# Activating the prompt's expert dot products in pairs on ScalarE, in the first of two PEER layers

## The chip, the cores and the metric

One core of a Trainium2 chip runs the whole program. The metric is the device time of one execution in microseconds (us). A slot, below, is one retrieved expert for each of 128 tokens; PE is TensorE, DVE is VectorE, ACT is ScalarE, POOL is GpSimd, SP is SyncE.

## What is computed

Two layers of a trunk run over five tiles of 128 tokens: four of the sample, one of the prompt. Each layer has a mixer (layer 0: HGRN2 and attention; layer 1: an RG-LRU block) and then a PEER retrieval. The change is in the retrieval of layer 0, which for a tile of 128 tokens and 8 heads computes

```
q = (xb @ w_q);  s1, s2 = q halves @ keys;  top 16 of the 16 x 16 sums -> eidx, g = softmax(sc)
act = gelu(einsum('thkd,td->thk', u[eidx], xb))
return einsum('thk,thkd->td', (g * act), v[eidx])
```

So each head and tile (a unit) has 16 slots. For a slot, a row of `u` and a row of `v` are gathered for every token, the dot product of the `u` row with the token is taken, its gelu times the gate weighs the `v` row, and the weighed rows are summed.

## The kernel before

All five engines run programs written out in order; there is no scheduler. 1280 slots (640 to a layer) go through the same pipeline, slot `g` being `g // 16` in units. In layer 0 slots 0 to 511 belong to the sample (8 heads x 4 tiles) and slots 512 (`SAMPLE`) to 639 (up to `SPAN` = 640) to the prompt, 16 to a head. Below, the stage is these 128 slots of the prompt, and "slot 26" means the 26th of the stage, g = 538.

For each slot POOL gathers 128 rows of 8 KB into one place of a ring (L1227). In the stage the ring has only 6 places, because the rest of it holds work of the next mixer; a place is free when PE has used it (`slot_free`). DVE takes the dot products (L1731, `dots`). ACT applies gelu (`gelu(g)`, L1315, `acts`). In the stage ACT then also multiplies by the gate (L1321, `prods`) and spreads the result on the diagonal of a 128 x 128 matrix (L1325, `diag`, four buffers); both are `weight(g)`. Outside the stage DVE makes the diagonal in one instruction (L1740). PE multiplies the diagonal with the gathered `v` rows and adds up in PSUM (L2062, 8 matmul instructions to a slot). In the stage PE takes slots in pairs: at every odd slot it runs `accumulate(g - 1)` and `accumulate(g)`, one after the other, each waiting for its own diagonal.

Between slots every engine runs background steps of the next mixer, each at a written slot number, in a generator called `background()`; a step due at slot g comes after that engine's own work of slot g. In the stage the background is:

- slots 0 to 8: the end of the last sample tile of layer 0 (ACT: `end_root_mean_square` L1259 at slot 4, `store_end` L1275 at slot 8; PE: `end_turn` L2001 at slot 7);
- from slot 9 to about 80: four blocks, n = 0 to 3, of the RG-LRU over the sample, 16 slots apart. PE multiplies the inputs (L2099) and the gates (L2118). ACT copies out the inputs (L1348, L1355; slots 13 and 15 of block 0), applies gelu to the gate branch (L1401; slots 18 and 21), sigmoid (L1367; slots 23 and 25), exp and tanh (L1376, L1377) and the first squares (L1384) at slot 26, the other squares at slot 28, and sqrt (L1390) at slots 29 and 30. Block n has the same steps 16n slots later. DVE multiplies, scans and forms the output (L1809 to L1846);
- slots 80 to 127: the projection of three sample tiles (PE L1975, two to eight k steps between pairs; its weights L1183 are loaded by SP as the scans let go of their room), and for each tile a residual (DVE L1631, L1633), root mean square (ACT L1250 to L1254, slots 87, 103 and 119), norm (DVE L1639 to L1645, a slot later), transposes (PE L1988, slots 89, 105 and 121), the copy of these (ACT L1268, slots 90, 106 and 122) and queries (PE L2014, slots 91 and 92, 107 and 108, 123 and 124).

An ACT instruction of a function that isn't in the loaded table set has an ACT_TABLE_LOAD before it. In this kernel gelu, sigmoid, exp (with tanh) and sqrt each bring one when another of the four ran before; copies, squares and multiplications bring none. ACT also computes the softmax's exp for each unit (`exponent`, L1297, at slot 5 of a unit in the stage).

Of the kernel before, what the change touches and what calls it, by code (L numbers as in the profile page):

```python
# [23 lines left out]
ACT = mybir.ActivationFunctionType  # L24
# [917 lines left out]
def unit_of(u):  # L942

    layer, v = divmod(u, HEADS * NB)
    return (layer,) + (divmod(v, SB) if v < HEADS * SB else (v - HEADS * SB, SB))
# [13 lines left out]
def ends_tile(u):  # L959
    layer, h, b = unit_of(u)  # L960
    return h == HEADS - 1


def ends_sum(u):
    layer, h, b = unit_of(u)
    return b < SB or h == HEADS - 1


def made_by_act(g):
    return SAMPLE <= g < SPAN  # L970


def diags_before(g):

    lo, hi = SAMPLE, SPAN
    by_act = min(max(g, lo), hi) - lo
    return by_act if made_by_act(g) else g - by_act
# [28 lines left out]
def route_steps(u):  # L1006

    return (2, 4, 6, 8, 10) if u < SB else (0, 1, 3, 5, 7)


def end_steps(u):

    return (1, 3, 4, 6, 7, 8) if u == HEADS * SB else (3, 7, 9, 12, 14, 15)


def trunk(nc, X, HY, HT, ident, iota16, io):
    def body(sb, ps, sem):
# [26 lines left out]
        dots, acts, prods = (sb(n, [P, 2 * TOPK]) for n in ("dots", "acts", "prods"))  # L1044
# [51 lines left out]
        dot_done, act_done, diag_v, diag_a, prod_done = (sem(n) for n in ("dot_done", "act_done", "diag_v", "diag_a", "prod_done"))  # L1096
# [44 lines left out]
        with nc.Block() as block:  # L1141
# [91 lines left out]
            def _(act):  # L1233
# [22 lines left out]
                def end_root_mean_square(e):  # L1256
                    b, n = e % NB, 2 * NB + e
                    act.wait_ge(added, add_of(e // NB * HEADS * NB + (HEADS - 1) * SB + b if b < SB else (e // NB + 1) * HEADS * NB - 1) + 1)
                    act.activation(HY[:, b, :], X[:, b, :], ACT.Square, accum_out=ss[:, n:n + 1]).then_inc(e_squared, 1)  # L1259
                    act.wait_ge(e_squared, e + 1)  # L1260
                    act.activation(rt[:, n:n + 1], ss[:, n:n + 1], ACT.Copy, scale=1.0 / D, bias=EPS).then_inc(e_shifted, 1)
                    act.wait_ge(e_shifted, e + 1)
                    act.activation(rt[:, n:n + 1], rt[:, n:n + 1], ACT.Sqrt).then_inc(e_rooted, 1)
# [7 lines left out]
                def store_end(e):  # L1271
                    b = e % NB
                    act.wait_ge(e_turned, e + 1)
                    for k in range(KD):
                        last = act.activation(HT[:, k, b * P:(b + 1) * P], qp[:, k * P:(k + 1) * P], ACT.Identity,  # L1275
                                              scale=AB1[:, 0, cond_of(b), k:k + 1], bias=AB1[:, 1, cond_of(b), k:k + 1])
                    last.then_inc(e_stored, 1)
# [17 lines left out]
                def exponent(u):  # L1295
                    act.wait_ge(top_ready, u + 1)
                    act.activation(expo[:, :], top[:, :], ACT.Exp, bias=negtop[:, 0:1],  # L1297
                                   accum_out=total[:, 0:1]).then_inc(exp_done, 1)

                def unpack(u):  # L1300
                    a = add_of(u)
                    act.wait_ge(slot_free, (u + 1) * TOPK)
                    act.wait_ge(added, a)
                    if u == HEADS * NB - 1:
                        act.wait_ge(l_y, KD)
                    for r in range(2):
                        for c in range(2):
                            last = act.activation(tmp[r * HALF:(r + 1) * HALF, c * 512:(c + 1) * 512],  # L1308
                                                  acc[acc_of(u)][c * HALF:(c + 1) * HALF, r * 512:(r + 1) * 512], ACT.Copy)
                    last.then_inc(unpacked, 1)  # L1310

                def gelu(g):
                    act.wait_ge(dot_done, g + 1)
                    j = g % (2 * TOPK)
                    act.activation(acts[:, j:j + 1], dots[:, j:j + 1], ACT.Gelu_apprx_tanh).then_inc(act_done, 1)  # L1315

                def weight(g):
                    u, j = g // TOPK, g % (2 * TOPK)
                    act.wait_ge(gate_ready, u + 1)
                    act.wait_ge(act_done, g + 1)  # L1320
                    act.activation(prods[:, j:j + 1], acts[:, j:j + 1], ACT.Copy,  # L1321
                                   scale=gate[:, u % 2, g % TOPK:g % TOPK + 1]).then_inc(prod_done, 1)
                    act.wait_ge(prod_done, diags_before(g) + 1)
                    act.wait_ge(slot_free, g - NDIAG + 1)
                    act.activation(diag[:, g % NDIAG, :], ident[:, :], ACT.Copy, scale=prods[:, j:j + 1]).then_inc(diag_a, 1)  # L1325
# [277 lines left out]
                    due = next(rest, None)  # L1603
                for g in range(SLOTS_IN_ALL):
                    u, s = divmod(g, TOPK)
                    gelu(g)
                    if made_by_act(g):
                        weight(g)
                    if s == end_steps(u)[0] and u and ends_sum(u - 1):
                        unpack(u - 1)  # L1610
                    if s == route_steps(u)[3] and u + 1 < UNITS:
                        exponent(u + 1)
                    if u and ends_tile(u - 1) and ends_sum(u - 1):
                        e = unit_of(u - 1)[0] * NB + unit_of(u - 1)[2]
                        if s == end_steps(u)[2]:
                            end_root_mean_square(e)
                        if s == end_steps(u)[5] and e < NB:
                            store_end(e)
                    while due is not None and due <= g:
                        due = next(rest, None)  # L1620
# [789 lines left out]
```

## Time and profile before

| what | us |
|---|---|
| timed runs, median (lowest, highest) of 3 | 4360.12 (4358.41, 4360.19) |
| the profiled execution | 4355.29 |
| its span, first to last instruction | 4353.6 |
| busy: PE, DVE, ACT, POOL | 3097.8, 3114.9, 1325.1, 1525.2 |
| DMA: mean rate over the span | 343 GB/s |

All queries below are of this one profiled execution; its times are counted from the span's start. A line of the timeline gives start, duration, engine and line, what is written from what, the count of instructions merged, and in brackets the idle time of the engine before it with what ended it. TensorE's granted clock is 1.00 for 2.4 GHz and 0.50 for 1.2 GHz. The stage lies between about 2130 and 2590 us.

### The profile page before, as it was taken

The numbers are of one execution on the slowest core, as the hardware profiler recorded it, in microseconds if no ns is written. First come the engines' busy times: TensorE is split into PE (matmuls) and PEld (weight loads), VectorE is DVE, ScalarE is ACT, GpSimd is POOL, SyncE is SP. The second block draws the span as 40 slices with busy tenths as digits, with TensorE's granted clock in tenths as the row PEclk, the third lists the DMA queues.
The fourth block names the chain that finished last, engine by engine and source line by source line (L and its number), as shares of the span: only waits on it lengthen the run. The fifth ranks groups of instructions, "written<-read, shape, count | busy, mean of one in ns | idle before, by whom it ended". The sixth has DMA issues, their size and how long they took to land.

```text
span 4353.6 us, 47679 instructions
## 1 busy us (share of the span) xinstructions
PE 3097.8 (71%) x15504; PEld 1117.7 (26%) x15504; DVE 3114.9 (72%) x7566; ACT 1325.1 (30%) x3008; POOL 1525.2 (35%) x1310
## 2 busy tenths in 40 slices
PE   7698887776667667666699786657566576666665
PEld 2266564221111111111133231122221211221111
DVE  6633333678878888788767677878779787778776
ACT  5432142222212222122467642232323322222111
POOL 0000000344444444444333334434344344434442
PEclk9899968898778878777799888788888898876766
DMA  8511002899999999999888999999999999999997
GB/s 332 202 38 42 34 1 106 325 364 420 420 421 420 417 411 412 410 411 411 346 326 304 361 361 392 420 394 416 387 398 407 392 419 420 421 410 417 418 410 313
DMA packets 227796, 1494.28 MB, mean 343 GB/s; under 512 B 25016, under 2 KB 48360, under 8 KB 55400
## 3 DMA queue, kind: packets, MB, share of 16 engines
q0 software_dynamic: 184320, 1342.26, 75.9%
q1 hardware_dynamic: 35364, 133.37, 8.1%
q10 hardware_dynamic: 7884, 15.87, 1.0%
q8 instruction: 111, 1.82, 0.2%
q14 instruction: 117, 0.96, 0.1%
HBM read 1488.02 MB, written 3.38 MB: 343 GB/s over the span
## 4 chain that ended last, share of the span: by engine, by line
DMA 30%; DVE 20%; PE 18%; issue 10%; ACT 4%; POOL 1%; DVEq 0%; ACTq 0%; POOLq 0%
DMA trunk_ring<-in_uv,trunk_index 27%; PE trunk_acc L2062 9%; DVE trunk_ring L1731 5%; DVE trunk_diag L1740 3%; DMA trunk_wbuf<-in_w_lru 2%; PE trunk_qp L1975 2%; POOL trunk_ring L1227 1%; PE trunk_qp L2099 1%; DVE trunk_onehot L1702 1%; DVE trunk_onehot L1706 1%; DVE trunk_pick L1709 1%; PE trunk_q L2099 1%; PE trunk_acc L2099 1%; DVE trunk_work L1667 1%; ACT L1315 1%
## 5 line engine op out<-in xcount | busy, mean ns | idle before, releaser
L2062 PE MATMUL trunk_acc<-trunk_ring,trunk_diag 64*64 64x512 f32 x10240 | 1717.6, 769 | 1045.1 <-DVE trunk_diag L1740 973.8
L1227 POOL DMA_INDIRECT trunk_ring<-in_uv,trunk_index x1280 | 1513.1, 1182 | 2304.3 <-PE trunk_acc L2062 1940.3
L1731 DVE CUSTOM_DVE_ANT_0 trunk_ring<-trunk_ring,HY 128x1024 f32<-128x1024 f32 x1280 | 1562.8, 1223 | 537.1 <-DMA trunk_ring<-in_uv,trunk_index 514.2
L1315 ACT ACTIVATE trunk_acts<-trunk_dots 128x1 f32<-128x1 f32 x1280 | 257.1, 202 | 2303.3 <-DVE trunk_dots L1731 2299.7
L2062 PEld LDWEIGHTS trunk_acc<-trunk_ring,trunk_diag 64*64 64x64 f32 x10240 | 337.2, 155 | 2248.5 <-DVE trunk_diag L1740 1930.4
L1740 DVE TENSOR_SCALAR trunk_diag<-ident,trunk_acts,trunk_gate 128x128 f32<-128x128 f32 x1152 | 396.5, 344 | 104.7 <-ACT trunk_acts L1315 104.6
L2021 PE MATMUL trunk_qp<-HT,trunk_wbuf 128*128 128x512 f32 x448 | 274.7, 697 | 0.0
L1315 ACT ACT_TABLE_LOAD x137 | 175.8, 1283 | 2.4
L1308 ACT ACTIVATE trunk_tmp<-trunk_acc 64x512 f32<-64x512 f32 x264 | 155.5, 589 | 6.1 <-PE trunk_acc L2062 3.2
L2021 PEld LDWEIGHTS trunk_qp<-HT,trunk_wbuf 128*128 128x128 f32 x448 | 72.9, 204 | 215.4 <-issue 215.4
L1975 PE MATMUL trunk_qp<-trunk_ring,HY 128*128 128x512 f32 x224 | 109.1, 621 | 0.0
L2099 PE MATMUL trunk_q<-HT,trunk_wbuf 128*128 128x128 f32 (+1 forms) x304 | 63.0, 367 | 60.8 <-DMA trunk_wbuf<-in_w_lru 60.8
L1731 DVE DVE_READ_ACCUMULATOR2_ANT trunk_dots<- 128x1 f32 x1280 | 105.7, 83 | 0.0
L2014 PEld LDWEIGHTS trunk_q<-HT,trunk_wbuf 128*128 128x128 f32 x768 | 97.6, 206 | 30.2 <-issue 28.9
L446 POOL COPY hgrn_Vm<-hgrn_V 64x640 f32<-64x640 f32 x8 | 5.7, 718 | 278.9 <-ACT hgrn_V L476 278.7
L1297 ACT ACT_TABLE_LOAD x80 | 102.6, 1283 | 1.4
L2014 PE MATMUL trunk_q<-HT,trunk_wbuf 128*128 128x128 f32 x768 | 101.7, 292 | 1.1 <-ACT HT L1268 1.1
L248 DVE TENSOR_TENSOR mod_w_lo<-mod_wmod,mod_w_hi 128x4096 fp32r<-128x4096 f32 x16 | 70.8, 4425 | 35.9 <-DMA HY<-in_norm_g 16.9
L289 PE MATMUL mod_modp<-mod_w_hi,mod_cond_hi 128*2 128x512 f32 x192 | 77.0, 401 | 14.2 <-ACT mod_w_hi L220 14.2
L1748 DVE TENSOR_TENSOR trunk_tmp<-trunk_tmp,trunk_G 128x1024 f32<-128x1024 f32 x66 | 80.6, 1222 | 5.3 <-ACT trunk_tmp L1308 5.3
L1750 DVE TENSOR_TENSOR X<-X,trunk_tmp 128x1024 f32<-128x1024 f32 x66 | 80.9, 1225 | 2.3
L835 DVE CUSTOM_DVE_ANT_0 att_LG<-att_A,att_band 128x384 f32<-128x384 f32 (+2 forms) x40 | 22.3, 558 | 83.5 <-PE att_A L892 83.5
(319 smaller groups left out, 3396.1 us busy)
## 6 DMA issues: line engine op xcount, KB each, us to landing
mod_wmod<-in_w_mod SPq DMA_DIRECT2D x16, 2048.0 KB, 8.0
trunk_wbuf<-in_w_q SPq DMA_DIRECT2D x24, 1024.0 KB, 9.2
trunk_ring<-in_uv,trunk_index POOLq DMA_INDIRECT x1280, 17.5
HT<-in_w_mod SPq DMA_DIRECT2D x8, 2048.0 KB, 8.3
trunk_wbuf<-in_w_lru SPq DMA_DIRECT2D x16, 1024.0 KB, 18.6
trunk_wbuf<-in_w_rg SPq DMA_DIRECT2D x8, 1024.0 KB, 14.3
hgrn_wqvg<-in_w_hgrn_qvg SPq DMA_DIRECT2D x4, 1536.0 KB, 6.3
hgrn_wfb<-in_w_hgrn_fb SPq DMA_DIRECT2D x4, 1024.0 KB, 4.9
```

Source lines behind the costliest of these rows:

```text
L1227: pool.indirect_dma_start(ring[:, slot, :], None, uv[:, :], bass.IndirectOffsetOnAxis(ap=index[:, u % 2, s:s + 1], axis=0), element_offset ...
L1297: act.activation(expo[:, :], top[:, :], ACT.Exp, bias=negtop[:, 0:1], accum_out=total[:, 0:1]).then_inc(exp_done, 1)
L1308: last = act.activation(tmp[r * HALF:(r + 1) * HALF, c * 512:(c + 1) * 512], acc[acc_of(u)][c * HALF:(c + 1) * HALF, r * 512:(r + 1) * 512 ...
L1315: act.activation(acts[:, j:j + 1], dots[:, j:j + 1], ACT.Gelu_apprx_tanh).then_inc(act_done, 1)
L1731: dve.tensor_tensor_reduce(u_rows, u_rows, HY[:, b, :], 1.0, 0.0, ALU.mult, ALU.add, dots[:, j:j + 1]).then_inc(dot_done, 1)
L1740: dve.tensor_scalar(diag[:, g % NDIAG, :], ident[:, :], acts[:, j:j + 1], gate[:, u % 2, g % TOPK:g % TOPK + 1], ALU.mult, ALU.mult).then_ ...
L1750: dve.tensor_tensor(X[:, b, :], X[:, b, :], tmp[:, :], ALU.add).then_inc(added, 1)
L1975: last = pe.matmul(dst[:, lo:lo + 512], HY[:, b, k * P:(k + 1) * P], weights_of(k)[:, lo:lo + 512], start=(k == 0), stop=(k == KD - 1), sk ...
L2014: last = pe.matmul(q0[:, half * P:(half + 1) * P], wq[:, k * 2 * P + half * P:k * 2 * P + (half + 1) * P], HT[:, k, b * P:(b + 1) * P], st ...
L2021: return pe.matmul(qp[:, half * LS:(half + 1) * LS], wq[:, k * 2 * P + half * P:k * 2 * P + (half + 1) * P], HT[:, k, 0:LS], start=(k == 0 ...
L2062: last = pe.matmul(acc[acc_of(u)][c * HALF:(c + 1) * HALF, r * 512:(r + 1) * 512], diag[rows, g % NDIAG, rows], ring[rows, slot, D + c * 5 ...
L2099: last = pe.matmul(psum(i), w[:, k * 2 * P + c * P:k * 2 * P + (c + 1) * P], HT[:, k, tokens], start=(k == 0), stop=(k == KD - 1), skip_gr ...
```

## The change

ACT's `gelu` gets a count `n`: it waits for the dot products of slots g to g + n - 1, activates n adjacent columns in one instruction and signals `act_done` n times. Outside the stage n is 1 and nothing changes. In the stage ACT does nothing for its own slot at an even slot; at an odd slot it runs one `gelu` over two columns and then `weight` for the even and for the odd slot. The background steps, `unpack`, `exponent` and the rest keep their places in the loop. A step due at an even slot of the stage now runs before the gelu and the weight of that slot instead of after. No other engine's program changes.

```
-                def gelu(g):
-                    act.wait_ge(dot_done, g + 1)
+                def gelu(g, n=1):
+                    act.wait_ge(dot_done, g + n)
                     j = g % (2 * TOPK)
-                    act.activation(acts[:, j:j + 1], dots[:, j:j + 1], ACT.Gelu_apprx_tanh).then_inc(act_done, 1)
+                    act.activation(acts[:, j:j + n], dots[:, j:j + n], ACT.Gelu_apprx_tanh).then_inc(act_done, n)
...
                 for g in range(SLOTS_IN_ALL):
                     u, s = divmod(g, TOPK)
-                    gelu(g)
-                    if made_by_act(g):
+                    if not made_by_act(g):
+                        gelu(g)
+                    elif g % 2:
+                        gelu(g - 1, 2)
+                        weight(g - 1)
                         weight(g)
```

## Rows read from the trace of the kernel before

**Rows 1.** Windows: the stage; length, busy PE, PEld, DVE, ACT, POOL, clock, DMA share, GB/s

```profile
2130.00:2590.00 460.00, 389.03 (x1677) 146.31 (x1678) 315.78 (x675) 286.92 (x627) 153.01 (x128) 0.90 0.89 333
```

**Rows 2.** Waits within the stage: engine, line, waited for: total us, times, longest

```profile
ACT trunk_acts L1315 <- DVE trunk_dots L1731: 110.5, 46, 7.3
...
PEld trunk_acc L2062 <- ACT trunk_diag L1325: 107.5, 38, 9.5
```

**Rows 3.** Group of instructions within the stage: count, busy us, mean ns, idle before

```profile
L1315 ACT ACT_TABLE_LOAD x28 | 35.9, 1283 | 0.5
```

**Rows 4.** Timeline of ACT in block 0, slots 26 and 27 of the stage

```profile
2224.92 1.28 ACT L1315 ACT_TABLE_LOAD   x1
...
2227.26 1.28 ACT L1376 ACT_TABLE_LOAD   x1
...
2235.91 0.20 ACT L1315 ACTIVATE trunk_acts<-trunk_dots 128x1 f32<-128x1 f32 x1
...
2236.54 0.40 ACT L1325 ACTIVATE trunk_diag<-ident,trunk_prods 128x128 f32<-128x128 f32 x1
```

**Rows 5.** Timeline of PE in block 0, from before slot 26 to slot 29

```profile
2225.99 5.42 PE L2099 MATMUL trunk_qp<-HT,trunk_wbuf 128*128 128x512 f32 x12
2231.34 1.09 PE L2062 MATMUL trunk_acc<-trunk_ring,trunk_diag 64*64 64x512 f32 x8
2236.99 1.98 PE L2062 MATMUL trunk_acc<-trunk_ring,trunk_diag 64*64 64x512 f32 x8 [4.56 <-ACT trunk_diag L1325]
2238.90 5.97 PE L2099 MATMUL trunk_qp<-HT,trunk_wbuf 128*128 128x512 f32 x12
2244.81 1.95 PE L2062 MATMUL trunk_acc<-trunk_ring,trunk_diag 64*64 64x512 f32 x16
```

**Rows 6.** Timeline of POOL, DVE, SP and PE in and behind block 3, to slot 84

```profile
2423.05 0.94 POOL L1227 DMA_INDIRECT trunk_ring<-in_uv,trunk_index  x1 [1.50 <-PE trunk_acc L2062]
...
2430.85 4.65 PE L2062 MATMUL trunk_acc<-trunk_ring,trunk_diag 64*64 64x512 f32 x24 [8.61 <-ACT trunk_diag L1325]
...
2442.20 1.22 DVE L1731 CUSTOM_DVE_ANT_0 trunk_ring<-trunk_ring,HY 128x1024 f32<-128x1024 f32 x1
...
2452.11 0.81 SPq L1183 DMA_DIRECT2D trunk_ring<-in_w_out  x2
...
2461.62 3.70 PE L1975 MATMUL trunk_qp<-trunk_ring,HY 128*128 128x512 f32 x8
```

**Rows 7.** DMA issues from 2400 to 2600 us: count, median us to landing

```profile
trunk_ring<-in_uv,trunk_index POOLq DMA_INDIRECT x63, 7.9
```

**Rows 8.** Timeline of PE at the second projected tile, slots 103 to 108

```profile
2517.72 1.99 PE L2062 MATMUL trunk_acc<-trunk_ring,trunk_diag 64*64 64x512 f32 x8 [2.45 <-ACT trunk_diag L1325]
...
2525.49 1.98 PE L2062 MATMUL trunk_acc<-trunk_ring,trunk_diag 64*64 64x512 f32 x8 [0.66 <-ACT trunk_diag L1325]
2527.41 1.97 PE L1988 MATMUL trunk_qp<-ident,HY 128*128 128x128 f32 x8
...
2531.40 1.09 PE L2062 MATMUL trunk_acc<-trunk_ring,trunk_diag 64*64 64x512 f32 x8 [0.59 <-ACT trunk_diag L1325]
2532.42 3.84 PE L2014 MATMUL trunk_q<-HT,trunk_wbuf 128*128 128x128 f32 x32
```

**Rows 9.** Timeline of ACT at the same tile: slots 103 and 105

```profile
2516.65 0.20 ACT L1315 ACTIVATE trunk_acts<-trunk_dots 128x1 f32<-128x1 f32 x1 [2.52 <-DVE trunk_dots L1731]
...
2517.58 1.04 ACT L1250 ACTIVATE HY<-X 128x1024 f32<-128x1024 f32 x1
...
2524.41 0.20 ACT L1315 ACTIVATE trunk_acts<-trunk_dots 128x1 f32<-128x1 f32 x1 [1.62 <-DVE trunk_dots L1731]
```

**Rows 10.** Windows of PE alone: start:end, length, busy (instructions), granted clock, DMA, GB/s

```profile
2517.00:2520.00 3.00, 1.99 (x8) 0.50 0.98 410
```

**Rows 11.** Timeline of DVE and ACT at the stage's entrance, slots 3 and 4

```profile
2143.08 1.23 DVE L1750 TENSOR_TENSOR X<-X,trunk_tmp 128x1024 f32<-128x1024 f32 x1
...
2146.41 1.04 ACT L1259 ACTIVATE HY<-X 128x1024 f32<-128x1024 f32 x1
```

## The prediction

> **What bounds the kernel now.** I read four views, all in the stage, since no program outside it changes. The windows: the stage is 460 us of the span, DMA busy at 0.89 and PE for 389 us [rows 1]. A wait taken out of it can therefore shorten it, and what is won or lost is kept, because the gathers behind the stage are issued as the ring comes free. The waits: PE's weight loads wait 107.5 us for ACT's diagonals, at 38 places, and ACT's gelu waits 110.5 us for DVE's dot products, at 46 [rows 2]. So PE hangs on ACT, but ACT has two reasons to be late: its own queue (then fewer instructions help) or a late dot product (then a gelu that waits for two dots makes the first of them later). The groups: in the stage gelu brings 28 table loads of 1283 ns, 35.9 us [rows 3], while one gelu takes 0.20 [rows 4]. The timeline of ACT and PE shows which reason holds where.
>
> **Part 1, what the pairs remove in an RG-LRU block (four times).** At slot 26 of block 0 the sigmoids are done when the gelu load begins at 2224.92. Gelu and weight of slot 26 follow, then the exp load at 2227.26. Exp, tanh and squares run, then a gelu load again, gelu 27 at 2235.91 and its diagonal at 2236.54 [rows 4]. In the change the exp step, due at the even slot 26, follows the sigmoids directly: no gelu load between, all 2227.26 - 2224.92 = 2.34 us earlier. The sqrt steps at slots 29 and 30 lose two more loads in the same way. That is three loads of 1.28 a block, 12 in all, 15.4 us of ACT.
>
> What reaches PE is less. Before, slot 26 was used at 2231.34, 4.56 us of idle followed, and slot 27 ran from 2236.99 [rows 5]. After, gelu for both starts at 2235.91 - 2.34 = 2233.57. The diagonal of 26 starts 0.63 behind it, as 2236.54 - 2235.91 shows, and ends 0.40 later at 2234.60; PE starts 0.05 after, at 2234.65. The diagonal of 27 costs a second `weight`, 0.64, and is hidden: PE needs about 1 us for slot 26. PE's idle shrinks only from 4.56 to 2234.65 - (2225.99 + 5.42) = 3.24, as slot 26 no longer runs ahead. Behind the idle before, 8 matmuls took 1.98 instead of 1.09 and the next 12 took 5.97 instead of 5.42: 1.44 lost to the lower clock [rows 5]. I take the same loss after 3.24 of idle. Both slots, the 12 matmuls and that loss, 1.88 + 5.35 + 1.44 with the overlaps of the rows taken off, end at 2243.3 to 2243.4; before it was 2244.81. Gain 1.4. Ends: 2.9 if the clock doesn't fall after the shorter idle; 0.3 if slots 26 and 27 both run at 1.98. From there PE is busy without a gap to the next block, so the two sqrt loads reach nothing. Blocks 0, 1 and 2 alike: **-4.2 (-8.7 to -0.9)**.
>
> Block 3 has no inputs of a next block behind it, so PE waits for ACT throughout and all three loads lie on that chain. But slot 74 is now used only with slot 75, and its place in the ring is let go late. Before, its gather (of slot 80) went out at 2423.05 [rows 6]. PE ran slot 75 from 2430.85, after 8.61 of idle [rows 6]; after, it starts 74 and 75 at 2430.85 - 2.34 = 2428.5, at 1.98 each, and the place of 74 is free at 2430.5, the gather out 0.8 later. Gathers here land after 7.9 us [rows 7], so 2439.2, just before DVE, whose work follows ACT's squares and moves with them, is free for slot 80 at about 2439.7; it was 2442.20. The last scans and outputs follow that dot, then the load of the last projection rows at 2452.11, then their matmuls at 2461.62 [rows 6]. So the end of block 3 gains at most 2.5, and nothing if the landing takes 3 us longer: **-1.8 (-2.6 to 0)**.
>
> A switch of tables here costs 1.28 and the next ACTIVATE follows directly [rows 4]. The Trainium skill (ScalarE: Activation LUTs, What ACT_TABLE_LOAD costs) adds about 1.38 us of drain to each. That drain is not visible in this trace; with it, three blocks would give an estimated 4.1 us more and the sum below would be about 0.7.
>
> **Part 2, what the pairs add at the projected tiles (three times).** Here ACT waits for dots, and the path runs through it: residual, root mean square, norm, transposes, copy, queries. The new wait is the gelu's for the odd dot; behind it on ACT are both weights and then the step of the tile, and PE's pair and POOL's gathers into the places of both slots wait for those. Three delays add up.
>
> First, ACT's L1250 followed the weight of slot 103 [rows 9]. Now two weights lie between the gelu at 2516.65 and L1250, +0.64, and DVE's norm and the dot of 105 wait for that. Second, slot 104, which PE had done before slot 105 (0.66 of idle between [rows 8]), now shares the gelu of 105. Gelu came at 2524.41 and PE at 2525.49, 1.08 later [rows 8, 9]; after, gelu at 2525.05, slot 104 on PE at 2526.13, slot 105 behind it, each 1.98 at the clock of these rows. The transposes start at 2530.0 instead of 2527.41: +2.6 so far. Third, the copy of the transposes is due at the even slot 106 and now precedes the gelu of 106. Slot 106, which ran in the shadow of the copy, follows it with slot 107 (was 2531.40), another +1.0 at full clock. The queries (2532.42) start 3.6 later. Behind them PE is busy on projections until the next tile, so the delay is kept. Ends: 2.7 if the longer run of slots 104 and 105 brings the clock back before the transposes (8 instructions in nearer 1.09 than 1.97 [rows 5, 8]); 5.4 if slots 106 and 107 run at 1.98 and the queries begin at the lower clock. Three tiles: **+10.8 (+8.1 to +16.2)**.
>
> PE idles longer in one piece here: from the end of slot 101 to the gelu of slot 103, where 102 used to run, and again up to 105. After 2.45 of idle slot 103 took 1.99, and the granted clock there was 0.50, the 1.2 GHz level [rows 8, 10]. The Trainium skill (TensorE: Matmul & The Clock Gate, HAM oscillation) warns that every idle gap before a burst may be paid again in slow matmuls; it speaks against this change, and by it the tiles stand at their upper end, which is rival (a).
>
> **Part 3, the entrance.** The root mean square at the even slot 4 waited for slot 4's weight until 2146.41, although its input was ready at 2143.08 + 1.23 = 2144.31 [rows 11]. It now starts 2.06 earlier; the exp and the gelus behind it follow until the dots of slots 5 and 7 limit them, so about 1.1 is left for PE. Against that, the copy at the even slot 8 now precedes slot 8's gelu, and slot 8 moves behind it with slot 9: +1.0 to +1.98 by the rows of the tiles [rows 8]. I take **0 (-1.1 to +1.7)**.
>
> **Nothing for the rest.** In the pairs where PE is busy without a gap, the first diagonal comes where the second used to and the second 0.64 later, behind 1 us of work for the first slot; the cover is PE's backlog, and without it each pair would cost about 1.0. A second column adds nothing that would show in a gelu's 0.20 [rows 4].
>
> **Sum.** -4.2 - 1.8 + 10.8 + 0 = +4.8. From the profiled 4355.29 that is 4360.1. The timed median is 4360.12, 4.8 above the profiled run; on it I forecast 4364.9.
>
> **Rivals.** (a) Slower: the low clock stays over slots 106 and 107 and the start of the queries in all three tiles. Then 16.2 + 1.7 - 4.2 - 1.8 = +11.9, 4372. It decides where slots 106 and 107 take over 3 us together instead of 1.95. For it: 1.98 at four places of one tile or block [rows 5, 8]. Against it: slot 107 already ran in 1.09, behind 0.59 of idle. (b) The change doesn't shed its loads, the gelu load before slot 26 staying where it was. Then 1.28 comes back at each of three blocks, which takes them to about -0.4, and the sum is +8.6 to +10: 4369. Against it: loads stand only where the set changes [rows 4]. (c) Faster: the tiles' delay is covered, because the projections between tiles wait for gathers and not for PE, and the blocks stay at full clock: -8.7 - 2.6 = -11.3, 4349. Against it: PE's rows there have no idle. For it: DMA at 0.89 over the stage [rows 1].
>
> **How the numbers follow.** Forecast 0.58, (a) 0.25, (b) 0.05, (c) 0.12. A measurement of this kernel tells about 0.2%, 8.7 us, from no change. The forecast lies within that, (a) and (b) beyond on the slow side, (c) on the fast side: 0.12 faster, 0.58 same, 0.30 slower. The range takes in the forecast's ends, which with all terms at one side would be -4.3 and +17, and case (a): 4355 to 4377. Only (c) lies outside.
>
> **What would show it.** Right: 20 gelu loads in the stage instead of 28 and four sqrt loads fewer; slots 26 and 27 as one run of 16 matmuls on PE behind some 3.2 of idle; at a tile, L1250 0.6 further behind its gelu, and the queries 3 to 5 us further behind the gelu of slot 103 than 2532.42 - 2516.65 = 15.77. Wrong: L1250 no later behind its gelu, slot 106 still ahead of the copy, or blocks that shorten by over 3 us each. Outside the stage, anything that moves by more than the shift would speak against all of it.

## The result: slower, and the profile after

| what | before | after |
|---|---|---|
| timed runs, median (lowest, highest) of 9 each | 4358.41 (4350.89, 4360.19) | 4377.3 (4372.27, 4400.12) |
| the profiled execution | 4355.29 | 4372.3 |
| its span | 4353.6 | 4370.6 |
| ACT: instructions, busy us | 3008, 1325.1 | 2932, 1292.2 |

After to before is 1.0047, with a 95% interval of 1.0034 to 1.0059: slower, by about 20 us. The forecast was 4364.9 (4355 to 4377), a change too small to be told from none. The profiled execution after is nearly the fastest of its nine, so the profiles differ by less, 17.0 us.

ACT lost what it was to lose: 76 instructions, 64 gelus and 12 table loads. The stage grew all the same, 18.0 us from its first scores to the last. These are lines of the profile after, windows, waits and groups of the stage, which answer to [rows 1 to 3] (line numbers behind L1312 are shifted by one to four).

```profile
2130.00:2610.00 480.00, 393.76 (x1692) 149.04 (x1696) 315.04 (x676) 253.33 (x550) 150.80 (x129) 0.90 0.86 320
```

```profile
PEld trunk_acc L2066 <- ACT trunk_diag L1326: 113.5, 49, 9.5
ACT trunk_acts L1316 <- DVE trunk_dots L1735: 95.5, 28, 7.7
...
ACT L1316 <- DVE trunk_dots L1735: 34.2, 8, 9.3
```

```profile
L1316 ACT ACT_TABLE_LOAD x20 | 25.7, 1283 | 34.4 <-DVE trunk_dots L1735 34.2
```

PE is as busy as before, in a stage that is 18 longer. The new line is the third of the waits: an entry of L1316 without a tile, the table load, which waits for the dot products eight times, 34.2 us. Before, the 28 loads had 0.5 us of idle ahead of them in all [rows 3].

Where the time went can be read off PE's scores (128 x 128 matmuls of `trunk_sc`), one set to a unit of 16 slots. Their distances, from the timelines of PE:

| us between scores | before | after | shift |
|---|---|---|---|
| entrance | 59.28 | 60.13 | +0.85 |
| block 0, block 1, block 2 | 64.49, 64.67, 64.69 | 63.22, 62.88, 63.21 | -4.54 |
| block 3; then projection and tile 1 | 59.31, 52.56 | 54.57, 65.59 | +8.29 |
| tile 2, tile 3 | 47.57, 47.57 | 54.20, 54.35 | +6.63, +6.78 |

The row with +8.29 parts at the end of the projection's last matmuls, 2465.32 before [rows 6] and 2462.35 after: block 3 with the projection lost 2.3, tile 1 lost 5.9. Outside the stage it is -1.6 ahead and +0.6 behind. The 1.6 is scatter: all kernels here run the same program up to the stage, and they reach its first scores between 2129.99 and 2139.19. Together: +17.0, the difference of the two spans.

The timeline of ACT in tile 2 after, beside [rows 9]:

```profile
2514.27 0.31 ACT L1297 ACTIVATE trunk_expo<-trunk_top,trunk_negtop 128x16 f32<-128x16 f32 x1
...
2519.66 1.28 ACT L1316 ACT_TABLE_LOAD   x1 [4.99 <-DVE trunk_dots L1735]
2520.95 0.20 ACT L1316 ACTIVATE trunk_acts<-trunk_dots 128x2 f32<-128x2 f32 x1
...
2522.51 1.04 ACT L1250 ACTIVATE HY<-X 128x1024 f32<-128x1024 f32 x1
...
2529.38 1.28 ACT L1316 ACT_TABLE_LOAD   x1 [4.00 <-DVE trunk_dots L1735]
2530.68 0.20 ACT L1316 ACTIVATE trunk_acts<-trunk_dots 128x2 f32<-128x2 f32 x1
```

The exp of `exponent` is over at 2514.7, ACT idles for 4.99 us, and only then, when the dot has come, the table is loaded. Before, the load ran right behind the exp, inside the idle:

```profile
2510.83 0.19 ACT L1297 ACTIVATION_READ_ACCUMULATOR trunk_expo<-trunk_top,trunk_negtop 128x1 f32 x1
2511.03 1.28 ACT L1315 ACT_TABLE_LOAD   x1
2513.11 0.20 ACT L1315 ACTIVATE trunk_acts<-trunk_dots 128x1 f32<-128x1 f32 x1 [0.79 <-DVE trunk_dots L1731]
```

The timeline of PE at the same tile after, beside [rows 8]: the pair 102 and 103, the pair 104 and 105, transposes, the pair 106 and 107, queries.

```profile
2522.03 3.44 PE L2066 MATMUL trunk_acc<-trunk_ring,trunk_diag 64*64 64x512 f32 x16 [6.02 <-ACT trunk_diag L1326]
2531.76 3.69 PE L2066 MATMUL trunk_acc<-trunk_ring,trunk_diag 64*64 64x512 f32 x16 [6.28 <-ACT trunk_diag L1326]
2535.38 1.09 PE L1992 MATMUL trunk_qp<-ident,HY 128*128 128x128 f32 x8
2538.50 3.50 PE L2066 MATMUL trunk_acc<-trunk_ring,trunk_diag 64*64 64x512 f32 x16 [2.03 <-ACT trunk_diag L1326]
2541.92 3.94 PE L2018 MATMUL trunk_q<-HT,trunk_wbuf 128*128 128x128 f32 x32
```

From the gelu of slot 103 to the transposes it is 14.43 (10.76 before), and from there to the queries 6.54 (5.01 before). From the queries of tile 1 (2487.82; before 2484.85) to that gelu it is 33.13 (31.80). So +1.33, +3.67 and +1.53, in all the 6.5 of this tile.

### The profile page after: what moved, and what is told of

Its sections match the earlier page's. It is cut to its first block, busy times and chain, and to the rows that moved or that the text cites. A ratio compares the mean times of both kernels' runs of the same rounds, so it can differ in the third digit from the quotient of the medians.

```text
span 4370.6 us, 47667 instructions
## 1 busy us (share of the span) xinstructions
PE 3107.1 (71%) x15504; PEld 1119.4 (26%) x15504; DVE 3114.5 (71%) x7566; ACT 1292.2 (30%) x2932; POOL 1526.1 (35%) x1310
## 4 chain that ended last, share of the span: by engine, by line
DMA 30%; DVE 21%; PE 17%; issue 11%; ACT 4%; POOL 1%; DVEq 0%; ACTq 0%; POOLq 0%; SPq 0%
DMA trunk_ring<-in_uv,trunk_index 28%; PE trunk_acc L2066 9%; DVE trunk_ring L1735 5%; DVE trunk_diag L1744 3%; DMA trunk_wbuf<-in_w_lru 2%; PE trunk_qp L1979 1%; POOL trunk_ring L1227 1%; PE trunk_qp L2103 1%; DVE trunk_onehot L1706 1%; DVE trunk_onehot L1710 1%; DVE trunk_pick L1713 1%; PE trunk_q L2103 1%; PE trunk_acc L2103 1%; DVE trunk_work L1671 1%; PE trunk_q L2018 1%
## 5 line engine op out<-in xcount | busy, mean ns | idle before, releaser
L1316 ACT ACTIVATE trunk_acts<-trunk_dots 128x1 f32<-128x1 f32 (+1 forms) x1216 | 244.5, 202 | 2284.2 <-DVE trunk_dots L1735 2282.8
L1316 ACT ACT_TABLE_LOAD x129 | 165.5, 1283 | 36.3 <-DVE trunk_dots L1735 34.2
L2103 PE MATMUL trunk_q<-HT,trunk_wbuf 128*128 128x128 f32 (+1 forms) x304 | 61.6, 362 | 61.5 <-DMA trunk_wbuf<-in_w_lru 61.5
```

The source lines that it names most:

```text
L1316: act.activation(acts[:, j:j + n], dots[:, j:j + n], ACT.Gelu_apprx_tanh).then_inc(act_done, n)
L2103: last = pe.matmul(psum(i), w[:, k * 2 * P + c * P:k * 2 * P + (c + 1) * P], HT[:, k, tokens], start=(k == 0), stop=(k == KD - 1), skip_gr ...
```

## The experiments

Twelve kernels, each timed in several rounds beside the kernel before; ratios are to that kernel, with their 95% intervals. "Distance" is that between scores, as in the table above. Two (e2_count_two, e6_half_rows_single) are the kernel before with one edit; the others are the kernel after, all but e1_count_one with pairs in some slots only, by this edit and a range for `paired`:

```
+def paired(g):
+    return made_by_act(g) and LO <= g - SAMPLE < HI
...
                     if not made_by_act(g):
                         gelu(g)
+                    elif not paired(g):
+                        gelu(g)
+                        weight(g)
                     elif g % 2:
```

### 1. Does the load behind the wait cost the time? (e1_count_one, e2_count_two)

The pair's gelu differs from the single one in two things: it has two columns, and it counts `act_done` up by two. e1_count_one keeps pairs and counts by one:

```
-    act.activation(acts[:, j:j + n], dots[:, j:j + n], ACT.Gelu_apprx_tanh).then_inc(act_done, n)
+    act.activation(acts[:, j:j + n], dots[:, j:j + n], ACT.Gelu_apprx_tanh).then_inc(act_done, 1)
...
-                    act.wait_ge(act_done, g + 1)
+                    act.wait_ge(act_done, acted(g))
```

`acted(g)` is the number of gelus up to that of slot g; DVE's two waits on `act_done` get it too.

> The changed kernel with one difference: a gelu of a pair counts act_done up by one instead of two, and the waits on act_done use the new count. In the built program the table load of a paired gelu then stands ahead of the wait for the dot again, as in the kernel before; pairs, their order and all other work stay. Theory (the loads moved behind the waits): in each of tiles 1 to 3 two loads of 1.28 us go back under the wait, so a tile costs 3.6 instead of 6.2 to 6.8 us against the kernel before, and the entrance about 1.3 less: 7.8 to 9.1 us faster than the changed kernel, about 4368 in the median, still slower than before by some 10. Rival (what the tiles lose is all lateness of the pair and the low clock of TensorE behind it; the loads are off the path): no difference to the changed kernel, 4377.

Measured: 4367.58, 1.0021 (1.0012 to 1.003); against 1.0047 that is 10 to 11 us back, and the intervals don't meet. Its ACT at tile 3, both loads of gelu and the gelus behind them:

```profile
2570.30 1.28 ACT L1326 ACT_TABLE_LOAD   x1
2575.29 0.20 ACT L1326 ACTIVATE trunk_acts<-trunk_dots 128x2 f32<-128x2 f32 x1 [3.70 <-DVE trunk_dots L1748]
...
2579.74 1.28 ACT L1326 ACT_TABLE_LOAD   x1
2583.67 0.20 ACT L1326 ACTIVATE trunk_acts<-trunk_dots 128x2 f32<-128x2 f32 x1 [2.65 <-DVE trunk_dots L1748]
```

The loads run first and the gelu waits. The distances of tiles 2 and 3 are 51.73 and 51.53: 4.2 and 4.0 over the kernel before, where the change has 6.6 and 6.8. So the loads behind the wait cost some 2.6 a tile, 7 to 8 us of the 20 if tile 1 is charged the same, and the rival (no difference) falls. In tile 1 itself only 1.1 came back in this profile, because its pair of slots 90 and 91 and its queries ran more slowly here (2.70 and 4.70 us) than in the change (1.95 and 3.84).

e2_count_two does the opposite: the kernel before, single slots, but a count of two (the waits on `act_done` use the new count).

```
-    act.activation(acts[:, j:j + 1], dots[:, j:j + 1], ACT.Gelu_apprx_tanh).then_inc(act_done, 1)
+    act.activation(acts[:, j:j + 1], dots[:, j:j + 1], ACT.Gelu_apprx_tanh).then_inc(act_done, 2 if made_by_act(g) else 1)
```

> The kernel before, single slots throughout, with one difference: a gelu of the stage counts act_done up by two instead of one, and the waits on act_done use the new count. In the built program all 28 table loads of gelu in the stage then stand behind the wait for the dot. Theory (a load behind a wait costs its 1.28 us only where TensorE's next work hangs on the very dot waited for): at a tile the load before slot 102 delays slot 102 alone, and slot 103, whose dot comes 3 us later, is not delayed; the load before slot 104 finds its dot ready. So the time between the scores of two tiles stays at 47.6 us and the kernel within 3 us of the kernel before. Rival (a load behind a wait costs 1.28 wherever it stands): 2.6 a tile, as with the pairs, and about 8 us or more in all.

Measured: 4358.31, 0.9997 (0.9988 to 1.0006); distances of the tiles 47.68 and 47.96. Its ACT at tile 2:

```profile
2513.42 1.28 ACT L1319 ACT_TABLE_LOAD   x1 [2.07 <-DVE trunk_dots L1735]
2514.71 0.20 ACT L1319 ACTIVATE trunk_acts<-trunk_dots 128x1 f32<-128x1 f32 x1
...
2516.97 0.20 ACT L1319 ACTIVATE trunk_acts<-trunk_dots 128x1 f32<-128x1 f32 x1 [1.24 <-DVE trunk_dots L1735]
```

Here, too, the load waits for the dot, so the count moves it, not the second column. But slot 103's gelu still waits 1.24 for its own dot behind it. With single slots the late load delays only slot 102, which has time. The load becomes dear only when slot 102's load stands in front of slot 103's gelu, and that is what the pair does.

### 2. Which slots lose, which gain? (e4_pairs_tiles, e3_pairs_blocks, e5_pairs_b02)

e4_pairs_tiles: `80 <= g - SAMPLE < 128`. e3_pairs_blocks: `0` to `80`. e5_pairs_b02: `0` to `64`. All count by two, as the change does.

> The changed kernel with pairs only in slots 80 to 127 of the stage (the projected tiles), single slots in the entrance and blocks 0 to 3. Theory: tiles 1 to 3 cost 6.2 to 6.8 us each, 19 us slower than the kernel before, about 4378. Rival, the sum on record: 3.6 each, 10.8 us slower. Second rival (the tiles lose this much only because block 3 handed them a queue of late gathers): under 10 us.

Measured: 4381.96, 1.0054 (1.0041 to 1.0067), 23 us; distances of tiles 2 and 3 54.58 and 54.60, +7.0 each, and +7.2 for the projection with tile 1. The tiles alone carry all of the loss; they lose it without the change in block 3.

> The changed kernel with pairs only in slots 0 to 79 of the stage (entrance, blocks 0 to 3), single slots in the projected tiles (80 to 127). Theory from the shifts between the two traces (entrance +1.4, blocks 0 to 2 -5.1, block 3 +2.3): 1.4 us faster than the kernel before, within 0.2% of it, and the projection of tile 0 ends no more than 2 us earlier. Rival, the sum on record (entrance 0, blocks -4.2, block 3 -1.8): 6.0 us faster.

Measured: 4359.36, 1.0001 (0.9992 to 1.001): the theory, not the sum on record, which would be 0.9986. Its tiles 2 and 3 take 47.57, as before. Blocks 64.48, 63.02 and 61.57, then 55.21 for block 3 (4.1 less than before) and 58.99 for the projection with tile 1 (6.4 more): block 3 wins 4.1 and gives back 6.4.

> The changed kernel with pairs only in slots 0 to 63 of the stage (entrance, blocks 0 to 2), single slots in block 3 and in the tiles. Theory (block 3 loses its gain because with pairs slot 74 is added up together with 75 to 77, so that its gather goes out 3 us later and the DMA engines run dry): with single slots the DMA engines stay fed and the gain of blocks 0 to 2 is carried through block 3: 3.7 us faster than the kernel before, about 4354.7, and 2.3 faster than pairs in slots 0 to 79. Rival (the projection's rows are bound by the DMA engines however block 3 is entered): no faster than pairs in slots 0 to 79, 1.4 us below the kernel before.

Measured: 4357.03, 0.9998 (0.9989 to 1.0006), not the 3.7 faster of the theory. Block 3 takes 59.31, exactly as before, but the projection with tile 1 takes 54.21, 1.65 more, although slot 74's gather goes out early again. So a late gather of slot 74 isn't all of it. Here slot 78 ran at the higher clock and its gather went out 5.1 behind the first rows (2437.47 to 2442.55), 6.0 in the kernel before (2434.86 to 2440.83); whether so little is enough wasn't tried. The next pair of runs asks whether the rows are bound by the DMA engines.

### 3. Are the projection's rows bound by the DMA engines? (e6_half_rows_single, e7_half_rows_pairs)

Both load only half of each row block of `w_out` and leave out the other half, so the projection's result is another and only the time counts: e6_half_rows_single in the kernel before, e7_half_rows_pairs in e3_pairs_blocks.

```
-    sp.dma_start(w_out[:, k, :], io["w_out"][1, k * P:(k + 1) * P, :]).then_inc(w1_in[k], 16)
+    sp.dma_start(w_out[:, k, 0:D // 2], io["w_out"][1, k * P:(k + 1) * P, 0:D // 2]).then_inc(w1_in[k], 16)
```

> The kernel before with half of the bytes of the last projection's rows (only the first 512 columns of each of the eight row blocks of w_out are loaded; the other half of the weights is left as it was, so the projection's result is another). A control for the same edit with pairs. Theory (the DMA engines bound the projection, but with single slots it just fits): from the scores behind block 3 to those of tile 1 51 to 52.5 us instead of 52.56, the kernel 0 to 2 us faster than the kernel before. Rival (the projection hangs on the rows here too): over 3 us faster.

Measured: 4356.67, 0.9994 (0.9985 to 1.0003); projection with tile 1 52.69 (before 52.56). With single slots the rows are no limit.

> Pairs in slots 0 to 79 as before, single slots in the tiles, and half of the bytes of the last projection's rows (only the first 512 columns of each of the eight row blocks of w_out are loaded, so the projection's result is another). Theory (pairs in block 3 bring the four gathers behind slots 74 to 77 to the queue together with the rows, and the DMA engines, empty for 4 us before, bound the projection): TensorE waits for rows no longer, the scores behind block 3 come 4 us earlier as with all rows (55 us after those before them instead of 59.3), and the scores of tile 1 no more than 53 us after them instead of 59.0; 4 to 6 us faster than the same kernel with all rows, about 4354. Rival (slots 80 to 83 wait for their gathers and the matmuls of the projection stand behind them, whatever the rows): 58 to 59 us, no faster than with all rows.

Measured: 4351.83, 0.9979 (0.997 to 0.9988); block 3 54.48, the projection with tile 1 55.14. PE in the last k steps of the projection, first with all rows (e3_pairs_blocks), then with half:

```profile
2448.73 1.96 PE L1986 MATMUL trunk_qp<-trunk_ring,HY 128*128 128x512 f32 x4 [1.82 <-DMA trunk_ring<-in_w_out]
2452.62 1.96 PE L1986 MATMUL trunk_qp<-trunk_ring,HY 128*128 128x512 f32 x4 [1.94 <-DMA trunk_ring<-in_w_out]
...
2460.34 1.95 PE L1986 MATMUL trunk_qp<-trunk_ring,HY 128*128 128x512 f32 x4 [1.81 <-issue]
```

```profile
2448.47 1.96 PE L1986 MATMUL trunk_qp<-trunk_ring,HY 128*128 128x512 f32 x4 [1.01 <-DMA trunk_ring<-in_w_out]
2451.63 1.95 PE L1986 MATMUL trunk_qp<-trunk_ring,HY 128*128 128x512 f32 x4 [1.20 <-DMA trunk_ring<-in_w_out]
...
2455.39 3.70 PE L1986 MATMUL trunk_qp<-trunk_ring,HY 128*128 128x512 f32 x8
```

Fewer bytes take 3.85 of the 6.4 out of the projection with pairs and nothing without them. So the rows bound the projection once block 3 is faster. They come late with half the bytes too (1.01, 1.20), so something else is in their way; that it is the gathers beside them is likely, but no run tested it. The 53 expected was missed by 2. By the two ratios the kernel as a whole gained 9.6 on e3_pairs_blocks, more than these 3.85, and where the rest is from stays open.

### 4. What else is in a tile? (e9_tiles_not_1011, e10_tiles_not_6to9)

Both count by one, with pairs in the tiles alone: e9_tiles_not_1011 without the pair of slots 106 and 107, e10_tiles_not_6to9 without those of 102 to 105 (and alike in the other tiles).

```
+    return made_by_act(g) and g - SAMPLE >= 80 and g % TOPK not in (10, 11)
...
+    return made_by_act(g) and g - SAMPLE >= 80 and g % TOPK not in (6, 7, 8, 9)
```

> Pairs only in the projected tiles (slots 80 to 127), but slots 10 and 11 of each unit of 16 (106 and 107 in tile 2) single again; act_done counted up by one by a pair, so that no load stands behind a wait. With all slots of the tiles in pairs and this count the time between the scores of two tiles was 51.6 us against 47.57. Theory (two shares: the late gelus of slots 102 to 105 cost 2.3 before the transposes and 0.4 before slot 102; the copy that now precedes slot 106 costs the rest): 47.57 + 2.7 = 50.2 us, some 9 us slower than the kernel before. Rival (the lateness up to the transposes is all of it, the copy is covered): 51.6 us.

Measured: 4361.88, 1.0008 (0.9999 to 1.0018); distances 49.89 and 49.42, 1.9 to 2.3 over before. The theory said 2.7, and 9 us for the kernel, of which the ratio shows some 3.

> Pairs only in the projected tiles (slots 80 to 127), but slots 6 to 9 of each unit of 16 (102 to 105 in tile 2) single; act_done counted up by one by a pair. Theory: the transposes come when they came in the kernel before, only the copy precedes slots 106 and 107, which costs 1.0 (the sum on record) to 1.5 (its share in the changed kernel): 48.6 to 49.1 us between the scores of two tiles, about 4 us slower than the kernel before. With the run without slots 10 and 11 the two shares add up to the 4.1 of all pairs. Rival (covered): 47.6 us.

Measured: 4368.63, 1.0025 (1.0016 to 1.0035); distances 51.12 and 51.18, 3.6 over before, where 1.0 to 1.5 was expected; the kernel is some 11 us slower than before, not 4. The two shares don't add up to the 4.1 of all pairs. PE of e10_tiles_not_6to9 at tile 2, transposes, slots 106 and 107, queries:

```profile
2538.02 1.97 PE L2004 MATMUL trunk_qp<-ident,HY 128*128 128x128 f32 x8
2542.01 3.69 PE L2078 MATMUL trunk_acc<-trunk_ring,trunk_diag 64*64 64x512 f32 x16 [2.03 <-ACT trunk_diag L1335]
2545.63 4.79 PE L2030 MATMUL trunk_q<-HT,trunk_wbuf 128*128 128x128 f32 x32
```

The order costs about 1.0, as the sum said (0.95 in tile 1 of the change, shown below). The rest is the clock: both slots run at the 1.2 GHz level (granted clock 0.50; 3.69, against 1.95 at 2.4 GHz), +1.7, and the queries begin there (4.79; before 3.84), +0.95. With all pairs (e1_count_one, tile 3) the clock comes back between: the transposes run in 1.09 instead of 1.97 and the queries in 3.93, which is why it is less there.

### 5. The blocks alone (e8_pairs_only_b02, e11_b02_count_two, e12_entrance_only)

e8_pairs_only_b02: slots 16 to 63, count of one. e11_b02_count_two: the same slots, count of two. e12_entrance_only: slots 0 to 15, count of two.

> Pairs only in slots 16 to 63 (blocks 0 to 2), act_done counted up by one by a pair, single slots in the entrance, block 3 and the tiles. Over the profiles of the four kernels with pairs in these blocks a block gained 0 to 3.1 us, 3.95 for the three on average, and the projection gave back 1.65. Theory: 2.3 us faster than the kernel before, about 4356, which a measurement hardly tells from it. Rival, the sum on record for these blocks with nothing given back: 4.2 faster. If the entrance with pairs cost 2 us, the time from the first scores to the next is about 57 to 59 us here and in the kernels with single slots, and about 60 in those with pairs.

Measured: 4352.17, 0.9984 (0.9975 to 0.9993): some 7 us faster than the kernel before, where 2.3 was expected, and faster than the change. Its profiled execution, 4343.67, is the fastest of its eleven.

> Pairs only in slots 16 to 63 (blocks 0 to 2), single slots in the entrance, block 3 and the tiles, as in the kernel that was 0.16% faster than before, but with act_done counted up by two by a pair, as in the change. Theory (in the blocks the dots are ready long before the gelu, so it costs nothing that a load stands behind the wait; what pairs in slots 0 to 15 cost is the entrance): as fast as with the count of one, 0.1 to 0.2% faster than the kernel before, and the first scores to the next in 57 to 58 us against about 60 with pairs in slots 0 to 15. TensorE's idle ahead of slots 26 and 27 is 3.25 in each block; if the granted clock behind it differs from block to block again, the block takes 61.6, 63.2 or 64.5 us with it. Rival (the count of one made the blocks faster): no faster than the kernel before.

Measured: 4351.67, 0.9985 (0.9975 to 0.9994). The count doesn't matter in the blocks, as the theory has it. But the entrance took 60.63, not the 57 to 58 of the theory.

> Pairs only in slots 0 to 15 of the stage (the entrance), act_done counted up by two by a pair, all other slots single. Pairs in slots 0 to 63 gave 0.02% less than the kernel before, pairs in slots 16 to 63 0.15% less. Theory (pairs in the entrance cost time of their own, the difference of the two, some 1.4 to 5 us): 0.03 to 0.12% slower than the kernel before, and the first scores to the next 60 us or a little more. Rival (pairs in the entrance cost nothing themselves, but move the blocks to where the clock falls behind the idle ahead of slots 26 and 27): as fast as the kernel before, blocks of 64.5 to 64.7 us, since blocks of single slots showed the lower clock in every profile so far. Second rival (on record: 0, with ends at -1.1 and +1.7): within 0.04%.

Measured: 4361.13, 1.0003 (0.9994 to 1.0012); entrance 61.70, blocks 64.7 each. It can't be told from no change. Over all profiles the entrance took 56.6 to 60.6 with single slots (mean 58.5) and 58.8 to 61.7 with pairs (mean 60.2), so its price, if any, is of that size and stays unsettled.

What the blocks gain hangs on the clock. PE behind the idle ahead of slots 26 and 27, first block 0 of e3_pairs_blocks, then block 0 of e8_pairs_only_b02:

```profile
2234.07 3.69 PE L2073 MATMUL trunk_acc<-trunk_ring,trunk_diag 64*64 64x512 f32 x16 [3.25 <-ACT trunk_diag L1330]
2237.70 6.59 PE L2110 MATMUL trunk_qp<-HT,trunk_wbuf 128*128 128x512 f32 x12
```

```profile
2229.57 1.95 PE L2079 MATMUL trunk_acc<-trunk_ring,trunk_diag 64*64 64x512 f32 x16 [3.25 <-ACT trunk_diag L1336]
2231.44 5.42 PE L2116 MATMUL trunk_qp<-HT,trunk_wbuf 128*128 128x512 f32 x12
```

The idle is the same 3.25, but until the next pair begins (2244.22, 2236.79) the 28 instructions take 10.2 in one and 7.2 in the other. A block takes 61.6 with no slow stretch, 62.9 to 63.2 with a short one, 64.4 to 64.5 with a long one. Of the 15 blocks in the five profiles with pairs in the entrance too, one took 61.6; of the six of e8_pairs_only_b02 and e11_b02_count_two, five. The means, 63.3 and 61.8 against 64.6 in the kernel before, make 4.0 and 8.3 for three blocks. That fits the 5 us between e5_pairs_b02 and these two kernels, though each kernel has one profile. What in the entrance decides the clock 60 us later, or whether the six are chance, was not settled.

## Why the prediction was wrong

| term | on record | profile after |
|---|---|---|
| blocks 0 to 2 | -4.2 (-8.7 to -0.9) | -4.5 |
| block 3, with the projection | -1.8 (-2.6 to 0) | +2.3 |
| entrance | 0 (-1.1 to +1.7) | +0.9 |
| three tiles | +10.8 (+8.1 to +16.2) | +19.4 |
| outside the stage | 0 | -1.0 |
| sum | +4.8 | +17.0 |

Two steps of the prediction failed. The sum of the tiles has no entry for the table loads, which the change itself put behind the waits, at some 7 to 8 us. And the last link of block 3 let the rows land as fast as before, so that 2.3 us were lost where 1.8 were to be won.

**Blocks 0 to 2: right, with their ends.** The timeline of PE in block 0 after, beside [rows 5]:

```profile
2225.56 5.42 PE L2103 MATMUL trunk_qp<-HT,trunk_wbuf 128*128 128x512 f32 x12 [0.28 <-DMA trunk_wbuf<-in_w_lru]
2233.89 2.68 PE L2066 MATMUL trunk_acc<-trunk_ring,trunk_diag 64*64 64x512 f32 x16 [2.91 <-ACT trunk_diag L1326]
2236.50 6.34 PE L2103 MATMUL trunk_qp<-HT,trunk_wbuf 128*128 128x512 f32 x12
2242.76 1.95 PE L2066 MATMUL trunk_acc<-trunk_ring,trunk_diag 64*64 64x512 f32 x16
```

Both slots in one run of 16 behind 2.91 of idle (3.25 in blocks 1 and 2; 3.24 predicted), and 1.65 of low clock (8.87 from there to the next pair, 7.22 at 2.4 GHz in e8_pairs_only_b02; 1.44 assumed). Both ends were met elsewhere: no slow stretch in e8_pairs_only_b02, both slots slow in block 0 of e3_pairs_blocks. So it is partly luck that -4.5 lies so near -4.2: the 1.44 was taken for every block, and the blocks of the experiments lost between nothing and 2.9 to the clock. Rival (b) falls: 20 gelu loads.

**Block 3: the last link failed.** Beside [rows 6], lines of POOL, DVE, SP and PE after:

```profile
2425.99 1.10 POOL L1227 DMA_INDIRECT trunk_ring<-in_uv,trunk_index  x1 [9.77 <-PE trunk_acc L2066]
...
2434.25 1.22 DVE L1735 CUSTOM_DVE_ANT_0 trunk_ring<-trunk_ring,HY 128x1024 f32<-128x1024 f32 x1
...
2444.15 0.81 SPq L1183 DMA_DIRECT2D trunk_ring<-in_w_out  x2
...
2448.92 1.96 PE L1979 MATMUL trunk_qp<-trunk_ring,HY 128*128 128x512 f32 x4 [1.74 <-DMA trunk_ring<-in_w_out]
2452.78 3.13 PE L1979 MATMUL trunk_qp<-trunk_ring,HY 128*128 128x512 f32 x4 [1.90 <-DMA trunk_ring<-in_w_out]
...
2458.18 1.98 PE L1979 MATMUL trunk_qp<-trunk_ring,HY 128*128 128x512 f32 x4
2460.39 1.96 PE L1979 MATMUL trunk_qp<-trunk_ring,HY 128*128 128x512 f32 x4 [0.22 <-issue]
```

The dot of slot 80 came 7.95 earlier than before, 2.6 more than the 5.3 that the blocks had won by then: the 2.5 of the step. The issue of the last rows moved with it (2444.15; before 2452.11). But their matmuls (2458.18; before 2461.62) came 14.0 behind that issue instead of 9.5. The step let the landing be as long as before, and that is what failed. Windows of 5 us, first before, then after; the DMA share is the last figure but one:

```profile
2430.00:2435.00 5.00, 4.15 (x24) 1.24 (x24) 3.05 (x7) 4.59 (x11) 1.46 (x2) 0.54 0.29 120
2435.00:2440.00 5.00, 1.95 (x16) 0.30 (x8) 4.96 (x8) 4.81 (x8) 3.23 (x2) 0.80 0.97 366
2440.00:2445.00 5.00, 2.19 (x12) 0.31 (x8) 4.89 (x8) 4.04 (x9) 0.94 (x1) 0.50 1.01 425
```

```profile
2420.00:2425.00 5.00, 1.80 (x12) 0.59 (x16) 3.34 (x6) 4.72 (x12) 0.00 (x0) 0.50 0.55 229
2425.00:2430.00 5.00, 3.28 (x28) 0.89 (x20) 5.00 (x10) 4.89 (x10) 3.40 (x3) 0.89 0.44 129
2430.00:2435.00 5.00, 2.77 (x16) 0.63 (x16) 4.90 (x6) 2.63 (x6) 3.29 (x3) 0.79 1.02 424
```

In both kernels the DMA engines run partly empty for want of free places and are then full, at about 425 GB/s. What differs is the queue ahead of the last rows. Before, the gather into slot 74's place had gone out ahead of the gap [rows 6], and five more went out from 2433.14 to 2445.63. After, seven went out from 2425.99 to 2443.00, four of them within 5 us, together with the first rows (from 2426.92). A gather is 128 rows of 8 KB, at 424 GB/s an estimated 2.5 us of all engines, so two more would be about 5 us; the matmuls came 4.5 later behind the issue. Experiment 3 bears this out in part, as half of the rows' bytes gave back 3.85. I had noted DMA busy at 0.89 [rows 1] and used it only for rival (c).

**Tiles: the term that was mis-sized.** Two things were wrong in it. First, the sum let the gelu start when its dot came, at 1.08 ahead of PE [rows 8, 9], and has no entry for the table load, because before it lay in the wait. Its place was not mine to assume: the change's own `then_inc(act_done, n)` moved it. That is 2.6 a tile, 7 to 8 us for the three (experiment 1). Second, the two delays that the sum does have, 2.6 ahead of the transposes and 1.0 behind them, measured 2.3 and 1.55 without the loads (e1_count_one, tile 3: gelu 2575.29, transposes 2588.37, queries 2594.93; before 10.76 and 5.01). The first is about what the sum has; the second is 0.5 more, by the clock. Tile 1 of the change shows it without that, transposes, slots 90 and 91, queries:

```profile
2481.86 1.97 PE L1992 MATMUL trunk_acc<-ident,HY 128*128 128x128 f32 x8
2485.94 1.95 PE L2066 MATMUL trunk_acc<-trunk_ring,trunk_diag 64*64 64x512 f32 x16 [2.12 <-ACT trunk_diag L1326]
2487.82 3.84 PE L2018 MATMUL trunk_q<-HT,trunk_wbuf 128*128 128x128 f32 x32
```

From the transposes to the queries it is 5.96, 0.95 more than the 5.01 before (2479.84 to 2484.85). In tiles 2 and 3 the pair took 3.50 and 3.24. The Trainium skill (TensorE: Matmul & The Clock Gate, HAM oscillation), which warns that each idle gap before a burst may be paid again in slow matmuls, agrees with tiles 2 and 3, where the pair was slow behind 2.03 of idle, and not with tile 1, where it ran in 1.95 behind 2.12.

Rival (a) was to be decided where slots 106 and 107 take over 3 us together. They did in two tiles of three, but (a) also had the queries at the lower clock, and they ran in 3.94 and 4.18 (3.84 before). Without the loads tiles 2 and 3 cost 4.2 and 4.0 (e1_count_one), nearer to the forecast's 3.6 than to (a)'s 5.4. So neither the forecast nor (a) had what made the difference: the loads, and the rows behind block 3. e1_count_one, the change without the loads, lies 9 us above the kernel before. That the +17.0 of the profiles is just the upper end of the range is chance, as neither of these two terms is in it. (c) falls with the sign. The last paragraph of the prediction had queries 3 to 5 us further behind the gelu of 103 than 15.77; they came 20.97, +5.2, and L1250 0.63 further behind its gelu, as said.

**Entrance:** +0.9 lies within its ends, and no run could price it better.

## What to carry to other kernels

When two waiting operations are merged, price not only that the first now waits for the second's input, but also what the first used to do while it waited: here a table load of 1.28 us that the wait had hidden. Look at the program as it is built, for whether a load, or any setup instruction, stands ahead of a wait or behind it. And let an engine's full stretches enter the sum: here a gain of 4.1 us ahead of a stretch with the DMA engines at 1.0 was more than given back there (6.4), and half of the rows' bytes saved 3.85 of that; earlier issues weren't tried. What paid was the part of the change where the removed load had stood in TensorE's way: pairs in blocks 0 to 2 alone are some 7 us faster than the kernel before (e8_pairs_only_b02, e11_b02_count_two).

## What was not expected of the hardware

- In these kernels a gelu that counts its semaphore up by two has its table load behind the wait; with a count of one the load stands ahead of it, with one column or two (2513.42 with 2.07 of wait ahead in e2_count_two; 2570.30 with none in e1_count_one).
- Behind the same 3.25 us of idle the granted clock fell in most blocks and not in others: 28 matmul instructions in 7.2 or in up to 10.2 us. In e8_pairs_only_b02 it fell in none of three blocks: it was 1.00 throughout from 2160 to 2405.
